# Token blocks of 368, 360 and 360 columns in place of 364, 362 and 362

## What is computed

```python
qa, ka, va, qb, kb, vb, qi, ki, wi, ga, gb = project(xp, g_pre_mix[l], w_in[l])   # rms_norm(x) @ w_in, 1024 -> 5064
...
def merge_and_mlp(x, o_a, o_b, g_a, g_b, w_o, g_post_mix, g_pre_mlp, w_up, w_down, g_post_mlp):
    mix = (jax.nn.sigmoid(g_a) * o_a + jax.nn.sigmoid(g_b) * o_b) @ w_o
    x = x + rms_norm(mix, g_post_mix)
    hid = jnp.square(jax.nn.relu(rms_norm(x, g_pre_mlp) @ w_up))      # 1024 -> 4096
    return x + rms_norm(hid @ w_down, g_post_mlp)                     # 4096 -> 1024
```

## Time and profile before

| | us |
|---|---|
| median of the three runs | 1902.87 |
| the profiled execution's own time | 1903.1 |
| its span, first to last instruction | 1901.3 |
| TensorE busy in the span | 1879.1 |
| granted TensorE clock, mean over the span | 0.998 of 2.4 GHz |

### The profile page before, as it was taken

One profiled execution on the slowest core, in us unless ns is written; L12 is line 12 of the kernel. 1 busy time (PEld: TensorE's weight loads), 2 busy tenths in 40 slices (PEclk: granted clock), 3 DMA queues, 4 the chain that ended last, 5 costly groups with the idle time before them and its releaser, 6 DMA issues.

```text
span 1901.3 us, 32833 instructions
## 1 busy us (share of the span) xinstructions
PE 1879.1 (99%) x11892; PEld 1778.6 (94%) x11892; DVE 1136.7 (60%) x2694; ACT 712.9 (37%) x1424; POOL 611.2 (32%) x493
## 2 busy tenths in 40 slices
PE   9999999999999999999999999999999999999997
PEld 8899999877778999999998889999999999999996
DVE  5259999999765667676664553333333333333336
ACT  5345554233345556555673442222222222222222
POOL 4225554134344334444341022222222222222223
PEclk9999999999999999999999999999999999999999
DMA  6433333233556444444323331111111111111114
GB/s 205 116 84 85 99 95 94 83 107 91 124 134 144 102 102 102 102 102 91 68 69 126 114 126 45 45 44 44 44 44 44 44 44 44 44 44 44 44 44 144
DMA packets 180398, 160.26 MB, mean 84 GB/s; under 512 B 101472, under 2 KB 148432, under 8 KB 180288
## 3 DMA queue, kind: packets, MB, share of 16 engines
q1 hardware_dynamic: 164816, 139.72, 25.9%
q10 hardware_dynamic: 15472, 19.09, 4.4%
HBM read 120.63 MB, written 39.27 MB: 84 GB/s over the span
## 4 chain that ended last, share of the span: by engine, by line
PE 93%; DVE 2%; DMA 0%; issue 0%; SPq 0%; ACT 0%; DVEq 0%
PE ps L1084 23%; PE ps L1906 20%; PE ps L2472 19%; PE ps L1806 11%; PE ps L1782 6%; PE ps L1764 5%; PE ps L2153 5%; PE ps L1056 2%; PE ps L2134 0%; PE ps L2000 0%; DVE y L2416 0%; PE ps L1111 0%; DVE probs L1692 0%; DMA m_in<-merged_scr 0%; DVE total L2396 0%
## 5 line engine op out<-in xcount | busy, mean ns | idle before, releaser
L2472 PE MATMUL ps<-hid_hi,weights 128*128 128x362 f32 (+1 forms) x1536 | 380.3, 327 | 0.0
L1906 PE MATMUL ps<-x2T_hi,weights 128*128 128x362 f32 (+1 forms) x1536 | 378.0, 326 | 0.0
L1906 PEld LDWEIGHTS ps<-x2T_hi,weights 128*128 128x128 f32 x1536 | 272.1, 188 | 0.1
L2396 DVE TENSOR_TENSOR total<-total,ps 128x362 f32<-128x362 f32 (+1 forms) x360 | 189.2, 532 | 138.5 <-PE ps L2472 138.5
L2472 PEld LDWEIGHTS ps<-hid_hi,weights 128*128 128x128 f32 x1536 | 270.4, 188 | 0.0
L1906 PE MATMUL ps<-x2T_lo,weights 128*128 128x362 f32 (+1 forms) x768 | 251.4, 327 | 0.0
L2472 PE MATMUL ps<-hid_lo,weights 128*128 128x362 f32 (+1 forms) x768 | 250.2, 326 | 0.0
L1084 PE MATMUL ps<-xT_hi,w 128*128 128x362 f32 (+1 forms) x960 | 246.1, 330 | 1.6 <-PEq L181 1.6
L2381 DVE TENSOR_TENSOR hidden<-hidden 128x362 f32<-128x362 f32 (+1 forms) x96 | 51.5, 537 | 293.5 <-ACT hidden L2356 293.5
L1893 POOL TENSOR_TENSOR weights<-down_raw,weights 128x512 fp32r<-128x512 f32 x64 | 83.8, 1312 | 380.6 <-ACT weights L1887 380.6
L1035 DVE MATCH_REPLACE8 score<-top,score 128x1024 f32<-128x1024 f32 (+5 forms) x208 | 199.3, 967 | 0.0
(11 more groups left out here) (200 smaller groups left out, 3332.8 us busy)
## 6 DMA issues: line engine op xcount, KB each, us to landing
q_raw<-q_scr SPq DMA_DIRECT2D x80, 256.0 KB, 5.0
w_raw<-in_w_in ACTq DMA_DIRECT2D x64, 256.0 KB, 3.0
up_raw<-in_w_up SPq DMA_DIRECT2D x64, 256.0 KB, 2.8
down_raw<-in_w_down SPq DMA_DIRECT2D x64, 256.0 KB, 2.6
gates<-gate_scr SPq DMA_DIRECT2D x34, 256.0 KB, 4.5
x_in<-in_x_prompt SPq DMA_DIRECT2D x16, 512.0 KB, 5.2
gate_scr<-stage SPq DMA_DIRECT2D x32, 256.0 KB, 3.1
q_scr<-stage SPq DMA_DIRECT2D x40, 181.0 KB, 3.1
```

Source lines behind the costliest of these rows:

```text
L1906: last = pe.matmul(ps[:, bank, 0:n], a[:, k, fs], b, start=(k == 0 and i == 0), stop=(k == KT - 1 and i == 2))
L2396: dve.tensor_tensor(out, out, more, ALU.add).then_inc(added, 1)
L2472: more = pe.matmul(ps[:, falling_bank(g, final), 0:n], a[:, f, cols], h, start=(f == 0 and i == 0), stop=(f == FT - 1 and i == 2))
```

## The change

The three blocks get other widths, and the two places that repeat the largest width follow. The sum is 1088 before and after, the number of matmuls and of all other instructions is unchanged, and so is their order.

```diff
@@ -384,7 +384,7 @@
-TOK_BLOCKS = [(0, 364), (364, 362), (726, 362)]
+TOK_BLOCKS = [(0, 368), (368, 360), (728, 360)]
@@ -1859,7 +1859,7 @@
-AFTER_TOTAL = UP_RAW_END + 4 * (2 * D + 2 * 364 + 2 * FT * N_QUERY + KT * N_QUERY)
+AFTER_TOTAL = UP_RAW_END + 4 * (2 * D + 2 * 368 + 2 * FT * N_QUERY + KT * N_QUERY)
@@ -2202,7 +2202,7 @@
-        hidden = sb("hidden", [P, 2, 364])
+        hidden = sb("hidden", [P, 2, 368])
```

## The result

| | before | after |
|---|---|---|
| time, median of 5 runs each, us | 1902.87 (1901.69 to 1903.76) | 1912.78 (1911.62 to 1913.4) |
| ratio to before, 95% interval | | 1.0052 (1.0037 to 1.0067) |
| span of the profiled execution, us | 1901.3 | 1911.6 |

The changed kernel is slower, by 9.9 us, and lies above the forecast of 1894 and above the range's end of 1907.

What follows compares the result with a forecast made beforehand. TensorE, busy 1879.1 of 1901.3 us, was taken to bound the kernel by its matmul pace. 1903.1 - 7.7 (MLP) - 1.0 (projection) = 1894.4 us, given as 1894; range 1889 to 1907, 8 in 10.

Steps and rivals of the forecast that it cites:

- What bounds the kernel: Whole kernel: TensorE is busy 1879.1 of 1901.3 us, so only the matmuls' start-to-start pace matters and no wait can go.
- MLP, blocks of 360 columns at 160.0 ns: MLP blocks 1 and 2, up and down products: 160.0 ns a matmul, 7.68 us for 48.
- The rule: Matmul pace: columns plus one cycle per 16, next start on a multiple of 16; 360 columns need 382, so 384.
- The price of the 24th piece: MLP, 362 columns: touching 24 rather than 23 pieces of 64 bytes raises 160.0 ns to 164.4 to 164.8.
- The bounds: MLP 360-column blocks: 160.0 ns as lower end, 163.3 ns from attention's 360 moving columns as upper.
- MLP, block of 368 at 166.7 ns: MLP block 0: 166.7 ns a matmul, 8.00 us for 48, as now; bounds 160.0 and 168 ns.
- The projection: Line 1084: groups of 24 at 3.94 us for 360 columns and 4.00 for 368, 1.0 us less in all.
- Everything else costs nothing: ScalarE's and VectorE's pieces, `q_scr` stores and waits: no cost; uncovered adds would differ by under 0.1 us.
- Nothing changes: Rival, chance 0.24: the columns' sum or position within 256 bytes decides; MLP gains 0, projection at most 1, 1902 us.
- Slower: Rival, chance 0.18: MLP blocks 1 and 2 run 360 at attention's pace, 6.7 us more there; 1909 us.

Runs made afterwards that it cites:

- pace_table: Matmul-only kernel, nothing of the layer computed: 135 pairs of width and first column, 48 matmuls each; 362 columns averaged 164.8 ns, 360 averaged 165.1.
- hidden_32_later: Kernel before, its widths kept, with `hidden` 368 instead of 364 columns wide, so the hidden columns start 32 bytes later; 1910.78 us, ratio 1.0048.
- products_in_turn: Matmuls alone, up, down, up, down, for five width triples at eight hidden-column places each; before's widths at place 96 took 47.21 us a pair.

## Why the prediction was wrong, step by step

*What bounds the kernel*: right. No wait came or went, and the time moved by what the pace of line 1906, 2472 and 1084 moved.

*MLP, blocks of 360 columns at 160.0 ns*: this step failed. They run at 166.5 to 166.7 ns, above the upper bound of 163.3 too. 64 blocks at 8.0 us where 7.68 was taken make 64 x 0.32 = 20 us; forecast and result lie 18.8 us apart. What the runs showed in its place: a block has no price by its width. The start addresses of its moving rows and of its weight tile and the matmuls before it choose a repeating pattern, and 360 columns from column 368 settled at 166.7 ns behind all sixteen forerunners. Two arguments stood behind the step, and both fell. The rule (columns plus one cycle in 16, up to the next 16) was made from three numbers and takes for a price what is a floor: none of the 135 cases of pace_table lies more than a cycle under columns plus a sixteenth, and on average they lie 12 cycles above; 358 and 360 columns need 380 and 382 cycles by it, and took 392 and 394.7 at column 0, and 360 took 400 at other columns. The price of the 24th piece was read from four blocks; over 33 starting columns it is 0.9 ns and not what separates 160 from 166.7.

*The bounds*: 163.3 ns was the pace of three matmuls in attention, behind other shapes. A block's pace depends on its addresses and forerunners, so a row from another stage bounds nothing here. Blocks of nearly this width in the same stage, the 364 wide one at 166.7 ns, should have been the upper end; with it the range would have reached 1903 + 16 x (0.42 + 0.38) = 1916.

*MLP, block of 368 at 166.7 ns*: 166.7 in the up and 165.6 in the down product, 0.05 us under the forecast for a block of 48 and just under the 166 of its own test. By the account above the value was no more secured than that for 360: in pace_table 368 columns took 166.7 to 173.3 ns.

*The projection*: 1.0 us less was forecast, 0.9 measured, partly by luck. Over all 60 groups block 2 gave 0.5 us where 0.2 was forecast and block 1 gave 0.8 as forecast, but block 0 cost 0.4 more where nothing was put. The three groups shown took 3.95, 3.95 and 4.02 us where 3.94, 3.94 and 4.00 were given.

*Everything else costs nothing*: right.

*The rivals*. "Nothing changes" named a true variable, the position, but supposed that it keeps its price when the widths and the forerunners change. "Slower" had the sign and the place, but the price of attention's row, 6.7 us in the MLP instead of 11.5, and its reason doesn't hold: 362 is not the one width that locks to 384 cycles. 354 and 356 columns took 160.0 ns at column 0, 360 took it at column 28, and 362 itself took it at only 4 of 33 starting columns. The linear rule of the Trainium skill, "TensorE: Matmul & The Clock Gate", section "Back-to-back issue gap", N / 2.4 plus 2.5 ns, would have given no change. It gives 153.3 ns for 362 columns, and 160.0 to 168.9 were measured. That section of the Trainium skill offers it as the gap of an isolated matmul and says that in a stream of weight loads and matmuls both set the spacing; the prediction left that out.

**Where the 11.5 us of the MLP come from.** In matmuls alone, before's pair lies 0.45 us under the mean of its eight places, the changed kernel's exactly at its mean, and the two means differ by 0.27. Counted against these means, 16 x 0.45 = 7.2 us is a favourable pattern given up, and 16 x 0.27 = 4.3 us goes with the widths. The real kernels allow another split, step by step: 16 x 0.54 = 8.6 us for the 32 bytes (hidden_32_later), then 16 x 0.18 = 2.9 us for the widths at the same place, 128. In the other order it comes out differently: by matmuls alone the widths at place 96 would cost 16 x 0.79 = 12.6 us, and the 32 bytes would then give some 1 us back. So the sum is shown, but no single share of it belongs to the place or to the widths.

**What stays open.** Why the paces settle on these values, and whether streams out of SBUF meet, and which. The table of places was taken within 256 bytes, and whether it repeats after 256 wasn't tried as such; but the real kernels at places 0 and 64 lie 256 bytes further on than the matmuls alone did, and their pairs agree.

## What to carry to other kernels

When a stage is nothing but matmuls back to back, its pace can depend on the moving width, on the start addresses of moving and weight tiles and on the matmuls before: the down product of 364, 362 and 362 columns took 23.36 us (place 224) to 24.21 (place 192) in products_in_turn, 4% apart for the same work. A model made from a few blocks doesn't extend to new widths; a matmul-only copy of the loop, with real addresses and real order, repeated for two turns, gave the pair of each of eight real kernels within 0.02 us. And an edit that also shifts a tile should be compared with that shift made alone, before its gain or loss is put down to the edit, and even then the two need not add up.

## What the runs showed of the hardware that wasn't expected

- A stream of equal matmuls settles into a repeating pattern. In pace_table 362 columns from column 364 start 160, 167, 168 and 165 ns apart, again and again from the first matmul to the last. The mean paces recur: 160.0, 163.3, 164.4, 166.7, 168.9, 173.3 ns, at 2.4 GHz 384, 392, 394.7, 400, 405.3 and 416 cycles, each a multiple of 16 cycles over one, two or three matmuls. About four in five of the 135 cases settle within 0.1 ns of such a value; others, such as the 165.0 ns above, repeat over more.
- More columns can be faster: 374 columns took 166.7 ns and 370 took 170 at the same start; 362 took 160.0 at column 2 and 166.7 at column 0.
- The same up and down products alternate between two speeds from chunk to chunk (24.15, 23.92, 23.84, 23.58 us), and a stream can have two outcomes at the same addresses (23.45 or 24.21 us), by what ran before.
